# Two transformer layers on one core: the weight-sum transfers of layer two are issued earlier, one after another

## The reference

```python
def second_block(...):
    h = concatenate([meta, x], axis=1)
    h = h + mixer_block(rms_norm_2(h, norm_mix), w_in, ..., w_out, lambda_init)
    h = h + swiglu(rms_norm_2(h, norm_ffn), w_ff_gate, w_ff_up, w_ff_down)
    return rms_norm_2(h, norm_final)[:, N_META:]

def swiglu(h, w_gate, w_up, w_down):          # 1024 -> 2816 -> 1024
    return (silu(h @ w_gate) * (h @ w_up)) @ w_down

def mixer_block(...):
    proj = h @ w_in                            # queries, keys, values, two gates
    y_a = differential_attention(...)          # softmax map 1 - lambda * softmax map 2
    y_b = windowed_gqa(...)
    merged = sigmoid(ga) * (y_a @ w_ba) + sigmoid(gb) * (y_b @ w_bb)
    return merged @ w_o
```

## Time and profile before

| | |
|---|---|
| median of 3 runs | 1472.45 us (1471.33 to 1475.7) |
| profiled execution | 1473.38 us, of which span 1471.7 us |
| PE busy | 1452.7 us, 99% |
| DVE / ACT / POOL busy | 975.2 / 654.3 / 258.2 us |
| granted TensorE clock, mean | 0.997 of full speed |
| DMA moved | 236.91 MB, mean 161 GB/s |

### The profile page before, as it was taken

One profiled execution on the slowest core, in us unless ns is written; L12 is line 12 of the kernel. 1 busy time (PEld: TensorE's weight loads), 2 busy tenths in 40 slices (PEclk: granted clock), 3 DMA queues, 4 the chain that ended last, 5 costly groups with the idle time before them and its releaser, 6 DMA issues.

```text
span 1471.7 us, 23871 instructions
## 1 busy us (share of the span) xinstructions
PE 1452.7 (99%) x8712; PEld 1253.2 (85%) x8712; DVE 975.2 (66%) x1779; ACT 654.3 (44%) x1175; POOL 258.2 (18%) x260
## 2 busy tenths in 40 slices
PE   9999999999999999999999999999999999999998
PEld 8868786888898898999899777777888988989997
DVE  6678977575776576787744372434767765867875
ACT  5234446535453353465411373544344533534643
POOL 2024536201101100000003675331011001000000
PEclk9999999999999999999999999999999999999999
DMA  7536674249899993663223237653388999736632
GB/s 187 148 100 211 173 133 130 79 111 191 202 328 226 250 217 98 199 184 106 86 86 86 58 101 162 151 188 80 107 186 226 305 218 242 213 95 195 185 104 93
DMA packets 342909, 236.91 MB, mean 161 GB/s; under 512 B 24729, under 2 KB 322837, under 8 KB 342814
## 3 DMA queue, kind: packets, MB, share of 16 engines
q1 hardware_dynamic: 305518, 152.24, 36.4%
q0 software_dynamic: 37216, 83.27, 24.8%
q10 hardware_dynamic: 80, 0.14, 0.0%
HBM read 233.48 MB, written 81.88 MB: 214 GB/s over the span
## 4 chain that ended last, share of the span: by engine, by line
PE 88%; DMA 6%; DVE 3%; ACT 1%; issue 1%; DVEq 0%; SPq 0%; POOL 0%; ACTq 0%
PE psL L2293 37%; PE psL L2520 12%; PE psS L2316 10%; PE psL L2316 6%; PE psS L2293 5%; PE psT L2316 4%; PE psT L2529 2%; DMA stage<-in_w_ffn_up 1%; DMA stage<-in_w_ffn_gate 1%; DMA stage<-in_w_ff_up 1%; PE psL L2655 1%; PE psS L2836 1%; PE psS L2570 1%; PE psL L2791 1%; PE psS L2814 1%
## 5 line engine op out<-in xcount | busy, mean ns | idle before, releaser
L918 ACT ACTIVATE wh<-stage 128x1024 fp32r<-128x1024 f32 (+3 forms) x211 | 203.6, 965 | 362.1 <-PE psL L2293 199.6
L1398 DVE TENSOR_TENSOR wl<-stage,wh 128x1024 fp32r<-128x1024 f32 (+2 forms) x168 | 183.8, 1094 | 57.7 <-ACT wh L918 57.3
L2293 PE MATMUL psL<-hid,wh 128*128 128x512 f32 x672 | 207.3, 390 | 0.0
L2520 PE MATMUL psL<-hn,wh 128*128 128x512 f32 x496 | 165.0, 414 | 0.8 <-DVE yn L2176 0.8
L2293 PE MATMUL psL<-hn,wh 128*128 128x512 f32 x528 | 165.0, 394 | 0.0
L2293 PEld LDWEIGHTS psL<-hid,wh 128*128 128x128 f32 x672 | 125.6, 188 | 26.2 <-DVE wl L1398 0.6
L2293 PE MATMUL psL<-hid,wl 128*128 128x512 f32 x336 | 130.7, 389 | 0.0
L746 POOL TENSOR_TENSOR wl<-stage,wh 128x1024 fp32r<-128x1024 f32 (+1 forms) x43 | 97.7, 2273 | 172.7 <-ACT wh L918 172.7
L2293 PEld LDWEIGHTS psL<-hn,wh 128*128 128x128 f32 x528 | 97.7, 188 | 23.1 <-issue 3.3
L2520 PEld LDWEIGHTS psL<-hn,wh 128*128 128x128 f32 x496 | 84.5, 189 | 24.5 <-issue 11.1
L2293 PE MATMUL psL<-hn,wl 128*128 128x512 f32 x264 | 102.9, 390 | 0.0
(11 more groups left out here) (507 smaller groups left out, 3333.0 us busy)
## 6 DMA issues: line engine op xcount, KB each, us to landing
stage<-in_w_in SPq DMA_DIRECT2D x53, 512.0 KB, 4.0
wsum<-weight_sums_1g SPq DMA_DIRECT2D x18, 512.0 KB, 5.2
wsum<-weight_sums_1u SPq DMA_DIRECT2D x18, 512.0 KB, 5.3
wsum<-weight_sums_2g SPq DMA_DIRECT2D x18, 512.0 KB, 4.7
wsum<-weight_sums_2u SPq DMA_DIRECT2D x18, 512.0 KB, 4.5
stage<-in_w_out SPq DMA_DIRECT2D x16, 512.0 KB, 4.7
stage<-in_w_ffn_down SPq DMA_DIRECT2D x32, 256.0 KB, 3.0
stage<-in_w_ff_down SPq DMA_DIRECT2D x32, 256.0 KB, 3.0
```

Of the source, the lines that this page charges most:

```text
L918: act.activation(wh[:, b, 0:n], stage[:, b, 0:n], ACT.Copy).then_inc(hi[b], 1)
L1398: v.tensor_tensor(wl[:, b, 0:n], stage[:, b, 0:n], wh[:, b, 0:n].bitcast(F32), ALU.subtract).then_inc(lo[b], 1)
L2293: ins = pe.matmul(dst, w[:, b, k * P:(k + 1) * P], x[:, part, k, c0:c1], start=done_ + n == 0, stop=done_ == kc - 1 and n == 2)
L2520: ins = pe.matmul(psL[:, b, :], w[:, b, k * P:(k + 1) * P], hn[:, part_, k, META:], start=k + n == 0, stop=k == KD - 1 and n == 2)
```

## The change

`sum_dmas` now counts transfers over all three parts of a layer and has a flag `one_by_one`: with it every transfer waits until all before it have landed. The transfers of layer two are issued at other places; those of layer one stay where they were.

```diff
-SUMS_AT = {1: (0, 2, 4, 6, 8, 10, 12, 14, 16), 2: (8, 10, 12, 14, 16, 19, 22, 24, 26)}
+SUMS_AT = {1: (0, 2, 4, 6, 8, 10, 12, 14, 16), 2: (30, 32, 34, 36, 38, 40, 41, 42, 43)}
...
-            def sum_dmas(l, part, first, last):
+            def sum_dmas(l, first, last, one_by_one=False):
...
-                    if before + n and (n in (0, 8, 12, 14) or 16 * part + n >= 24):
-                        pool.wait_ge(sums_in, 16 * (before + n))
+                    if before and (one_by_one or step in (0, 8, 12, 14)):
+                        pool.wait_ge(sums_in, 16 * before)
...
-            feed_sums(1)
+            feed_sums(1, SUM_DMAS + 8)
+            pool.wait_ge(mm[0], PAIR0["dn1b"])
+            sum_dmas(2, 0, 8, one_by_one=True)
+            pool.wait_ge(mm[0], PAIR0["dn1c"])
+            sum_dmas(2, 8, 16, one_by_one=True)
...
             pool.iota(dist[:], pattern=[[-1, DIST]], base=3 * P, channel_multiplier=1,
                       allow_small_or_imprecise_dtypes=True).then_inc(dist_ok, 1)
+            sum_dmas(2, 16, 22, one_by_one=True)
...
                 if u % 2 == 0:
-                    sum_dmas(2, 0, u // 2 - 1, u // 2)
-            sum_dmas(2, 0, 7, 8)
+                    sum_dmas(2, 21 + u // 2, 22 + u // 2, one_by_one=True)
+            sum_dmas(2, 29, 30, one_by_one=True)
             for i in range(PAIRS["gates2"]):
                 low_pair("gates2", i)
-                part = SUMS_AT[2][i] // SUM_DMAS
-                sum_dmas(2, part, SUMS_AT[2][i] - part * SUM_DMAS, SUMS_AT[2][i + 1] - part * SUM_DMAS)
-            feed_sums(2)
+                sum_dmas(2, SUMS_AT[2][i], SUMS_AT[2][i + 1])
+            feed_sums(2, SUMS_AT[2][-1])
```

More of the change, by code:

```diff
@@ L750, in low_pair @@
                 low(name, i, 1)
-            def sum_dmas(l, part, first, last):
[L754 to L758, removed]
-                for n in range(first, last):
-                    if before + n and (n in (0, 8, 12, 14) or 16 * part + n >= 24):
-                        pool.wait_ge(sums_in, 16 * (before + n))
-                    m = "gu"[n % 2]
+            def sum_dmas(l, first, last, one_by_one=False):
+                for n in range(first, last):
+                    before = SUM_DMAS * len(FPARTS) * (l - 1) + n
+                    part, step = divmod(n, SUM_DMAS)
+                    t0, t1 = summed_pairs(part)
+                    cols = slice(t0 * P, t1 * P)
+                    second = slice((FPAIRS + t0) * P, (FPAIRS + t1) * P)
+                    upper, lower = slice(0, D // 2), slice(D // 2, D)
+                    if before and (one_by_one or step in (0, 8, 12, 14)):
+                        pool.wait_ge(sums_in, 16 * before)
+                    m = "gu"[step % 2]
                     w, s12, s43 = w_ffn[l, m], w_sums[l, m, 0], w_sums[l, m, 1]
@@ L766, in sum_dmas @@
                                (s12[upper, cols], w[lower, second]), (s43[lower, cols], w[upper, second]),
-                               (s12[lower, cols], s43[lower, cols]), (s43[upper, cols], s12[lower, cols]))[n // 2]
-                    if n < 8:
+                               (s12[lower, cols], s43[lower, cols]), (s43[upper, cols], s12[lower, cols]))[step // 2]
+                    if step < 8:
                         pool.dma_start(to, src).then_inc(sums_in, 16)
@@ L805, in _ @@
                     low_pair("gates1", i)
-                sum_dmas(1, 0, SUMS_AT[1][i], SUMS_AT[1][i + 1])
+                sum_dmas(1, SUMS_AT[1][i], SUMS_AT[1][i + 1])
             def mask_bias(j):
@@ L814, in mask_bias, with feed_sums @@
                 pool.tensor_tensor(biasM[:, j % 4, 0:K], biasB[:, h, NKEY - K:NKEY], selm[:, i, 0:K], ALU.subtract).then_inc(biasM_ok, 1)
-            def feed_sums(l):
+            def feed_sums(l, first):
                 pool.wait_ge(mix_ok, KD * l)
-                sum_dmas(l, 1, 8 if l == 1 else 10, SUM_DMAS)
-                sum_dmas(l, 2, 0, SUM_DMAS)
+                sum_dmas(l, first, SUM_DMAS * len(FPARTS), one_by_one=True)
             la_units = list(latent_units())
@@ L828, in _ @@
                 if j % 4 == 3:
-                    sum_dmas(1, 1, j // 4, j // 4 + 1)
-            feed_sums(1)
+                    sum_dmas(1, SUM_DMAS + j // 4, SUM_DMAS + j // 4 + 1)
+            feed_sums(1, SUM_DMAS + 8)
[3 more added lines that the diff above has]
+            sum_dmas(2, 8, 16, one_by_one=True)
             pool.wait_ge(ev[1], PAIR0["kv2"] + 1)
```

## The result

| | before | after |
|---|---|---|
| median of 6 runs each | 1472.08 us (1469.54 to 1475.7) | 1484.89 us (1482.95 to 1488.33) |
| ratio, 95% interval | | 1.0095 [1.0077, 1.0114] |
| profiled execution (span) | 1473.38 us (1471.7) | 1488.32 us (1486.6) |
| granted TensorE clock, mean | 0.997 | 0.992 |

The account below looks back on a forecast made before the run. TensorE's own work was taken as the bound (88% of the span), with GpSimd having no slack before `gates2`. Terms -2.0 + 0.3 + 0 + 11.5 + 1.7 = +11.5 us on 1472.45 gave 1484 us; 8-in-10 range 1476 to 1493.

Parts of the forecast that it names:

- `gu2a`, -2.0: Layer two's `gu2a`: fewer sum transfers left after `mix_ok`, so its half entries lose no time to late loads; -2.0 us.
- `dn1b`, +0.3: Transfers 0 to 7 beside `dn1b`: 5.2 us each, the last reaching into `gu1c`'s loads; +0.3 us, bounds 0 and +6.2.
- upper bound of +6.2: Most that transfers 0 to 7 in `dn1b` might cost, taken from what `gu1b` lost in all.
- third rival: Crowding in layer one: transfers 0 to 7 at 7 us spoil `gu1c`'s first entries; up to 6.2 more, 1490 us; chance 0.09.
- `dn1c` and `kv2`, 0: Transfers 8 to 15 in `dn1c` and 16 to 21 in `kv2` stay hidden: 0 us, upper bound +10.
- the cover: In `kv2`: time hiding six copies before the copy of the values and `qa2`'s `wl`; ends at 6.8 us a transfer.
- df, +11.5: Df attention: adding transfers 24 to 29, each waiting 7.3 us, delay `wl` and TensorE's start on `gates2`; +11.5 us, ends +9.3, +26.4.
- The `m8d` copies: Df attention: copies queued behind waiting transfers, the last 5.8 us later; inside the 11.5 us, adding nothing.
- the prediction's own sign: First `gates2` quarter: TensorE idle of 10 us or more ended by `wl`; prediction wrong if idle before `gates2` under 6 us.
- The clock, +1.7: After TensorE's standstill before `gates2`, one stretch partly at 1.2 GHz; +1.7 us, bounds 0 and 3.4.
- first rival: Df attention: adding transfers land within GpSimd's slots, only 29 waits; +1.4, 1474 us, not slower; chance 0.12.

Follow-up runs that it names:

- e6: Kernel after, with copies 16 to 23 unwaited in df attention, 24 to 31 in `gates2`, 32 to 47 all after `mix_ok`; 1470.86 us, ratio 1.0013.
- e7: Kernel after, with copies 16 to 23 unwaited in df, 24 to 40 in `gates2`, `dn1c`'s wait dropped so 8 to 15 run into `gu1c`; 1469.62 us, 0.9998.
- e10: Kernel after, with copies 16 to 23 unwaited in df, 24 to 40 in `gates2`, layer one's 1024 KB adding transfers cut in two; 1466.04 us, 0.9956.
- e11: Kernel before, with only layer one's eight adding transfers of 1024 KB cut into two of 512 KB each; 1468.61 us, ratio 0.9969.
- e8: Kernel after, with nine one-by-one transfers (16 to 24) in `kv2`, none in df, 25 to 42 in `gates2`; 1477.71 us, ratio 1.0044.
- e1: Kernel after, but transfers 22 to 29 in df wait only at 24 and 28, same places in GpSimd's list; 1475.07 us, ratio 1.0012.
- e2: Kernel after, with transfers 28 and 29 moved behind the first `low_pair` of `gates2`, 22 to 27 still waiting; 1473.49 us, ratio 1.0000.
- e3: Kernel after, with transfers 24 to 29 moving half their bytes, leaving half of those sums out; 1477.09 us, ratio 1.0032.
- e9: e4 with each of layer one's eight adding transfers of 1024 KB cut into two of 512 KB; 1465.16 us, ratio 0.9941.
- e4: Kernel after, with copies 16 to 23 unwaited in df, 24 to 40 in `gates2`, layer one's adding 24 to 26 before `br1`; 1470.55 us, ratio 1.0000.

## Why the prediction was right, step by step

It said 1484 us and slower; 1484.89 was measured. The forecast difference was +11.5 us; the medians differ by 12.8, and the profiles by 13.0 beyond the 1.9 us that are not the change's. The terms:

- **`gu2a`, -2.0.** Measured -2.09, and e6 shows the cause: putting the transfers back behind `mix_ok` brings the loss back.
- **`dn1b`, +0.3.** Measured 0 (-0.01 in the table). The copies went out 4.3 to 5.0 us apart, not 5.2; the last was issued at 595.11, before `gu1c` began. The DMA share rose from 0.40 to 0.78 and TensorE stayed full. The upper bound of +6.2 came from `gu1b`, whose crowding comes with adding transfers of 1024 KB and goes when they are cut, as the text of the third rival suspected and e7 with e10 and e11 showed.
- **`dn1c` and `kv2`, 0.** As forecast: the sixth copy of `kv2` was issued at 773.48 (forecast 768 to 774) and the copy of the values at 779.81, its place plus the 1.9 us that after was late already. e8 put a number on the cover: with three transfers more it is gone.
- **df, +11.5.** Measured 13.05, the term with the largest error. The 7.3 us in it stood on one transfer's landing, with 10.0 as the other row; the reason for taking the shorter (nothing else loads there) held, but it was one row. The mechanism was right in every link (e1: without the waits 5.35 instead of 15.1 us in all, 1.6 of the 5.35 being the clock in `kv2`; e2: without the last two slots 2.43; e3: with a short landing only the last link costs much). Mis-sized was the distance between issues: 7.3 us was 7.43 to 7.69 (over five, 37.69 instead of 36.5, +1.2); and 24 was issued 0.3 us behind its place.
- **The `m8d` copies** behind the waiting transfers did stop TensorE, for 6.06 us; as the prediction had it this is inside the df term, since 29 comes later still. But it spoils the prediction's own sign. It wanted an idle time of 10 us or more before the first quarter of `gates2`, and called itself wrong under 6 us: there were 5.34 us. The standing came in two pieces, 6.06 and 5.34, because TensorE had met the queued copy first and then did its work between them slowly. The mechanism is the forecast one and the sum of the pieces (12.17 us) fits; the sign should have been set on that sum.
- **The clock, +1.7.** Measured 2.06, of which 0.2 are a longer wait before `out2`. About the same appears in the two other kernels where TensorE had stood for 5 us before `gates2` or `qa2`: 2.37 in e3, about 2.1 in e8. In e1, where the longest wait was 2.50 us, it is 1.6 us, all of it before `gates2`. In after the first wait had cost as much, but the second wait hid it. The size was in part luck: the row that it was taken from, at the beginning of `kv2`, shows 0, 1.6 or 3.1 us from execution to execution.

The Trainium skill (DMA: Bandwidth & Descriptors, Anatomy of one DMA) fits a transfer's time with about 2.0 us and its bytes at 436 KB per us; my estimate from it is 3.8 us for 768 KB, which would have given the first rival. In this stretch the two copies landed in 4.7 and 4.6 us and the adding transfers in 7.1 to 7.4: the trace disagrees for both, most where it adds. e3 shows that the rival was priced too low even on its own terms: with a landing of 5.3 us the kernel is 4.3 us slower than before, where 1.4 had been worked out, because the last link made `gates2` 4.4 us late instead of 3.4, and after that wait the clock fell.

Not settled: whether e9 is better than e10, why the same instructions meet a low clock in `kv2` in some executions and not in others, and whether a transfer's size or its packets' starve the loads beside it.

## What to carry to other kernels

An engine that issues transfers and computes in one list of instructions pays for a wait on a landing with everything queued behind it. Before making transfers wait for each other, compare one landing of that very kind (adding or copying, this size) with the work that stands between two issues; where it is longer, the excess adds up, and the last link, right before something TensorE needs, costs whole. And where TensorE starves beside a full DMA, look at the largest single transfer before moving anything: here moving it moved the stall (e4), and cutting it through the columns removed it in `gu1b` and most of it in `gu1a`.

## What the runs showed of the hardware that was not expected

- A DRAM-to-DRAM transfer that adds costs far more time than one that copies, with no other load about: 768 KB landed in 7.1 to 7.4 us against 4.6 to 4.7, and 384 KB in 5.2 to 5.4. The adding one moved 768 KB in 528 packets, the copy in 192. From those two sizes, each further 384 KB costs about 1.9 us and the fixed part is about 3.4 us (my estimate, by a line through two points).
- At the same DMA share (1.11 and 1.13) TensorE was busy for 18.77 of 21 us beside adding transfers of 1024 KB and for all 21 beside ones of 512 KB; loads of 256 KB took 7.5 to 10.0 us on the mean beside the first and 6.7 to 7.4 beside the second. A table of shares alone doesn't show such crowding; TensorE's busy time does, and the landing times less clearly.
- Standing still for 5 us cost TensorE another 2 us or so afterwards, most of it at 1.2 GHz, in three kernels (2.06, 2.37, 2.1); a wait of 2.5 us 1.6. Short waits of 0.8 us in all at the beginning of `kv2` cost 0 in two profiles, 1.6 in ten and 3.1 in two.
